# A streaming-encoder layer on one core: x handed over by columns, token sums loaded one by one, eight transpositions ahead of the first projection

## The chip, the core and the metric

One NeuronCore of a Trainium2 chip runs the whole program. TensorE (PE) multiplies, VectorE (DVE) and ScalarE (ACT) convert and do elementwise work, GpSimd (POOL) builds constants and issues some DMAs, SyncE (SP) issues nearly all loads. The metric is the time of one execution on the device in microseconds, the median of several.

## What is computed

One trunk layer on 256 tokens of 2048 columns, all in float32, cut to the lines that matter:

```python
h = rms_norm(x, attn_norm_w)                    # x: (1, 256, 2048)
proj = h @ w_in                                 # 2048 x 5184
hq, hf, hi, hg, c_q, c_kv, k_r = split(proj)    # 4 x 1024, 512, 512, 64
o_a = hgrn2_mixer(hq, hf, hi, hg, ...)          # gated linear recurrence, chunks of 64
o_b = mla_mixer(c_q, c_kv, k_r, ...)            # rms_norm(c_q) @ w_uq, rms_norm(c_kv) @ w_ukv, attention
x = x + concat([o_a, o_b]) @ w_out
gate, up = split(rms_norm(x, ffn_norm_w) @ w_gate_up)   # 2 x 5632
x = x + (silu(gate) * up) @ w_down
```

## The kernel before

**Products in three parts.** Every weight tile is loaded as float32 into `raw`, a ring of four granules. ScalarE rounds it to `w_hi` (line 793, in the later stages line 1013), VectorE takes the rest, `w_lo` = `raw` - `w_hi` (lines 1122 and 1573). The tokens are kept the same way, as `hT_hi` and `hT_lo`, columns on partitions. TensorE then adds hi x hi, hi x lo and lo x hi. For one 128-row tile of weights and 256 tokens these are six products; a granule of the first block (384 columns, two tiles of rows) takes twelve.

**Order.** The first 137 granules go through `w_in`, `w_uq`, `w_ukv` and `w_out`. A table, `SCHEDULE`, gives each side step (transposes, norms, attention) a position among the granules. Each engine walks through the granules and does its part of the steps that stand at a position; ScalarE and VectorE convert granule g + 3 (`LEAD`) at position g. SP loads granule g as soon as the ring slot of granule g - 4 has been converted. Everything on an engine runs in program order, so a wait on one step holds up all behind it.

**The start.** x lies in memory by rows (tokens on partitions). SP loads it in nine pieces, piece p of `PIECES` with its one or two tiles of columns, in turn with the granules 0 to 8 (`load_x`, line 567; weights, line 621); piece 1 and `attn_norm_w` go through ScalarE's queue. TensorE turns each piece by transposes into a `side` bank (`turn_x`, line 1773); ScalarE makes `hT_hi` from the bank with the norm weight as scale (line 840), VectorE makes `hT_lo` (line 1143). The norm weights come as rows and are turned too (`vec`, line 1787): the first 16 at the start, the other 25 at position 19. In the first block (`lat`, 0) the products (line 1751) wait separately for `w_hi` and `hT_hi`, for `hT_lo`, and for `w_lo`. The squares of x (`sq1`) stand at positions 3 to 9 and the root `r_in` at 10 and 11; the latents are multiplied by `r_in` as they leave the accumulation bank (`lat_in`, line 1237). POOL builds masks and other constants after the last piece of x has come (line 711).

**The down projection.** A feed-forward tile is either plain ("S": one granule, twelve products of 512 columns) or paired ("Q": two weight loads that become four granules with 3, 6, 6 and 6 products, and that need sums of token tiles). `DOWN_ITEMS` begins with five S and then repeats Q S S. The token sums were written to memory during the gate-up rounds; POOL loads them back (`sums_in`, line 768), two at a time into `chunk_of(c)`, in the former place of `hT_lo`. ScalarE and VectorE split them behind items 4, 9, 15, 21 and 27. On POOL's queue chunk 0 comes first, then the last turn of the hidden values through memory (`squares`, `hiddenT`, lines 749 and 755), then the other four chunks, each with this wait:

```python
            def sums_in(c):
                pool.wait_ge(s_used, W1 + 2 * c)
                for n, p in enumerate(CHUNKS[c]):
                    pool.dma_start(...)
```

`s_used` counts the granules that TensorE has used up, and `W1` is the first one of the down projection.

Of the kernel before, what the change touches and what calls it, by code (L numbers as in the profile page):

```python
# [27 lines left out]
ALU = mybir.AluOpType  # L28
# [32 lines left out]

V_ATTN, V_FFN, V_QN, V_KVN, V_HG, V_ROWS = 0, KT, 2 * KT, 2 * KT + 4, 2 * KT + 8, 2 * KT + 9
# [107 lines left out]
PAIRED_OF = [[i for i in DOWN_OF[e] if DOWN_ITEMS[i][0] == "Q"] for e in range(2)]  # L170
CONVERTED = AHEAD
# [45 lines left out]
def schedule():  # L217
# [56 lines left out]
    s += [(e + 3, ("r2a",)), (e + 4, ("r2b",))]  # L274
    return sorted(s, key=lambda x: x[0])
# [17 lines left out]
def split_steps_at(position):  # L293

    own = [step for step in steps_at(position) if step[0] != "x"]
    return own + [("x", p) for p, at in enumerate(X_SPLIT) if at == position]


def side_uses(step):

    kind = step[0]
    if kind in ("x", "x2", "lat_t", "o_t"):
        return [(step, "dve")]
    if kind in ("vec", "turn", "probs_t", "join7", "join8"):
        return [(step, "act")]
# [56 lines left out]
def hybrid_layer(nc, x, positions, attn_norm_w, w_in, hgrn_lb, hgrn_norm_w, mla_q_norm_w, w_uq, mla_kv_norm_w,  # L362
                 w_ukv, q_head_norm_w, k_head_norm_w, w_out, ffn_norm_w, w_gate_up, w_down, out):
# [6 lines left out]
    with ExitStack() as ctx:  # L370
# [14 lines left out]
        vec_cols = sb("vec_cols", [P, V_ROWS])  # L385
# [45 lines left out]
        vec_rows = stage[0:KT, 0, 0, 0, 0:P]  # L431
        more_rows = stage[0:V_ROWS - KT, 0, 0, 1, 0:P]
# [62 lines left out]
        s_x = [sem(f"s_x{p}") for p in range(len(PIECES))]  # L495
        s_attn = sem("s_attn")
# [66 lines left out]
        def load_x(engine, p):  # L563

            k, wide = PIECES[p]
            cols = slice(P * k, P * (k + wide))
            engine.dma_start(X[:, :, cols], x_v[:, :, cols]).then_inc(s_x[p], 16)
# [24 lines left out]
        def all_of(v):  # L592
# [3 lines left out]
        small_loads = [(more_rows[r - KT:r - KT + w.shape[1] // P, :], w.rearrange("a (k p) -> (a k) p", p=P))  # L596
                       for r, w in ((V_FFN, ffn_norm_w), (V_QN, mla_q_norm_w), (V_KVN, mla_kv_norm_w),
                                    (V_HG, hgrn_norm_w))]
        small_loads += [(pos_i[:, :], positions[0].rearrange("(t p) -> p t", p=P)),
                        (qw_row[:, :], q_head_norm_w[0].partition_broadcast(P)),  # L600
                        (kw_row[:, :], k_head_norm_w[0].partition_broadcast(P))]
# [6 lines left out]
        def _(sp):  # L608
# [5 lines left out]
            load_x(sp, 0)  # L614
            for g, (b, k, n) in enumerate(GRANULES):
                kind, i, w, c0, cols, rows, _ = BLOCKS[b]
                if g >= RING:
                    slot_free(g)
                src = weights[w][rows[k]:rows[k] + n * P, c0:c0 + cols].rearrange("(k p) c -> p k c", p=P)
                dst = raw[:, g % RING, 0:n * cols].rearrange("p (k c) -> p k c", k=n)  # L620
                sp.dma_start(dst, src).then_inc(s_raw[g % RING], 16)

                for p in X_AFTER.get(g, ()):
                    load_x(sp, p)

                if 0 <= g - 7 < N_SMALL:
                    dst, src = small_loads[g - 7]
                    sp.dma_start(dst, src, allow_slow_non_contiguous=True).then_inc(s_small, 16)
# [51 lines left out]
        def _(pool):  # L680
# [29 lines left out]
            pool.wait_ge(s_x[len(PIECES) - 1], 16)  # L710
# [73 lines left out]
        def _(act):  # L784
# [58 lines left out]
            def step(s):  # L843
                kind, a = s[0], s[1:]
                if kind == "vec":
                    lo, hi = ((0, KT), (KT, V_ROWS))[a[0]]
                    copy(vec_cols[:, lo:hi], filled(s)[:, 0:hi - lo]).then_inc(s_given["act"], 1)
                    act.wait_ge(s_given["act"], GIVEN[USE[s]])
                elif kind == "x":
                    ps, (k, wide) = filled(s), PIECES[a[0]]  # L850
                    split_hi([(hT_hi[:, k + n, :], ps[:, n * SEQ:(n + 1) * SEQ], V_ATTN + k + n) for n in range(wide)])
                elif kind == "sq1":
                    c = a[0]
                    for p, (k, _) in enumerate(PIECES):
                        if k // 4 == c:
                            act.wait_ge(s_x[p], 16)
# [8 lines left out]
                elif kind == "lat_a":  # L865
# [3 lines left out]
                    sums_free(s)  # L869
# [177 lines left out]
            for g in range(FIRST, G0):  # L1047
# [3 lines left out]
                for s in split_steps_at(g):  # L1051
                    step(s)
# [1037 lines left out]
```

## Time and profile before

| | us |
|---|---|
| median of 3 runs | 1115.05 (1113.57 to 1115.18) |
| the profiled execution | 1115.01 |
| its span, first to last instruction | 1113.3 |
| TensorE busy | 1103.5 (99%) |
| VectorE, ScalarE busy | 900.2 (81%), 644.7 (58%) |
| DMA | 230.01 MB, mean 207 GB/s |

A busy TensorE is not yet one at its best pace, since products overlap in the pipeline and their ends are modelled: how long a product really takes is the distance from its start to the next one's. The chain of waits follows the work that ended last back from the end. A wait is put down to what ended it, and idle time of an engine off the chain costs nothing by itself.

### The profile page before, as it was taken

The numbers are of one execution on the slowest core, as the hardware profiler recorded it, in microseconds if no ns is written. First come the engines' busy times: TensorE is split into PE (matmuls) and PEld (weight loads), VectorE is DVE, ScalarE is ACT, GpSimd is POOL, SyncE is SP. The second block draws the span as 40 slices with busy tenths as digits, with TensorE's granted clock in tenths as the row PEclk, the third lists the DMA queues.
The fourth block names the chain that finished last, engine by engine and source line by source line (L and its number), as shares of the span: only waits on it lengthen the run. The fifth ranks groups of instructions, "written<-read, shape, count | busy, mean of one in ns | idle before, by whom it ended". The sixth has DMA issues, their size and how long they took to land.

```text
span 1113.3 us, 15363 instructions
## 1 busy us (share of the span) xinstructions
PE 1103.5 (99%) x5176; PEld 927.6 (83%) x5176; DVE 900.2 (81%) x1234; ACT 644.7 (58%) x910; POOL 61.0 (5%) x154
## 2 busy tenths in 40 slices
PE   8999999999999999999999999999999999999998
PEld 7988888888888888888888888888888878888887
DVE  6688787587876577588988888988988889999887
ACT  7566777668654466365455555554554555655553
POOL 4200000000000000000000000000000020000000
PEclk9999999999999999999999999999999999999999
DMA  8766455554655455767777777787777786666665
GB/s 269 209 187 200 146 169 157 157 162 152 230 183 172 164 176 171 227 218 224 234 236 225 228 233 220 230 240 218 233 237 228 233 290 210 200 215 202 197 205 170
DMA packets 107557, 230.01 MB, mean 207 GB/s; under 512 B 8265, under 2 KB 19314, under 8 KB 107250
## 3 DMA queue, kind: packets, MB, share of 16 engines
q1 hardware_dynamic: 101346, 209.30, 60.3%
q0 software_dynamic: 5856, 19.93, 5.7%
q8 instruction: 28, 0.46, 0.2%
q14 instruction: 23, 0.19, 0.0%
q10 hardware_dynamic: 304, 0.14, 0.0%
HBM read 218.85 MB, written 10.49 MB: 206 GB/s over the span
## 4 chain that ended last, share of the span: by engine, by line
PE 91%; DVE 4%; DMA 2%; ACT 1%; issue 1%; SPq 0%; DVEq 0%; ACTq 0%
PE side L1975 22%; PE main L1731 20%; PE side L1977 11%; PE main L1734 10%; PE side L1945 4%; PE side L1946 4%; PE side L1947 4%; PE main L1945 3%; PE main L1946 3%; PE main L1947 3%; DMA raw<-in_w_down 1%; PE main L1751 1%; PE side L1773 1%; DVE w_lo L1122 1%; PE side L1870 1%
## 5 line engine op out<-in xcount | busy, mean ns | idle before, releaser
L1013 ACT CAST w_hi<-raw 128x1024 fp32r<-128x1024 f32 x245 | 239.8, 984 | 162.8 <-PE side L1975 62.8
L1573 DVE TENSOR_TENSOR w_lo<-raw,w_hi 128x1024 fp32r<-128x1024 f32 x245 | 274.6, 1133 | 17.7 <-ACT w_hi L1013 17.5
L1122 DVE TENSOR_TENSOR w_lo<-raw,w_hi 128x1024 fp32r<-128x1024 f32 (+3 forms) x156 | 178.8, 1156 | 97.1 <-ACT w_hi L793 94.4
L793 ACT CAST w_hi<-raw 128x1024 fp32r<-128x1024 f32 (+3 forms) x156 | 153.4, 993 | 130.2 <-PE main L1731 125.4
L1731 PE MATMUL main<-w_hi,hT_hi 128*128 128x512 f32 (+2 forms) x416 | 161.2, 388 | 0.2 <-issue 0.2
L1734 PE MATMUL main<-w_hi,hT_lo 128*128 128x512 f32 (+2 forms) x416 | 157.6, 380 | 0.0
L1975 PE MATMUL side<-w_hi,hT_hi 128*128 128x512 f32 x400 | 155.6, 389 | 0.0
L1977 PE MATMUL side<-w_hi,hT_lo 128*128 128x512 f32 x400 | 155.6, 389 | 0.0
L1731 PE MATMUL main<-w_lo,hT_hi 128*128 128x512 f32 (+2 forms) x416 | 107.1, 379 | 0.0
L1975 PE MATMUL side<-w_lo,hT_hi 128*128 128x512 f32 x400 | 106.9, 389 | 0.0
L1731 PEld LDWEIGHTS main<-w_hi,hT_hi 128*128 128x128 f32 x416 | 78.2, 188 | 13.2 <-issue 0.4
L1734 PEld LDWEIGHTS main<-w_hi,hT_lo 128*128 128x128 f32 x416 | 78.2, 188 | 12.9
L1731 PEld LDWEIGHTS main<-w_lo,hT_hi 128*128 128x128 f32 x416 | 76.8, 188 | 14.1
L1975 PEld LDWEIGHTS side<-w_lo,hT_hi 128*128 128x128 f32 x400 | 75.1, 188 | 15.6
L1977 PEld LDWEIGHTS side<-w_hi,hT_lo 128*128 128x128 f32 x400 | 75.1, 188 | 15.6
L1975 PEld LDWEIGHTS side<-w_hi,hT_hi 128*128 128x128 f32 x400 | 75.1, 188 | 15.6
L1573 DVE TENSOR_TENSOR w_lo<-last_two,w_hi 128x1024 fp32r<-128x1024 f32 x39 | 47.8, 1225 | 41.1 <-ACT w_hi L1013 41.1
L1013 ACT CAST w_hi<-last_two 128x1024 fp32r<-128x1024 f32 x39 | 41.0, 1052 | 63.9 <-PE side L1975 63.1
L1013 ACT CAST w_hi<-first_two 128x1024 fp32r<-128x1024 f32 x39 | 41.2, 1056 | 58.7 <-PE side L1975 58.1
L1975 PE MATMUL side<-w_hi,aT_hi 128*128 128x512 f32 x184 | 71.6, 389 | 0.0
L1977 PE MATMUL side<-w_hi,aT_lo 128*128 128x512 f32 x184 | 71.6, 389 | 0.0
L1731 PE MATMUL main<-w_hi,mT_hi 128*128 128x512 f32 (+1 forms) x160 | 62.0, 387 | 0.0
(292 smaller groups left out, 1887.5 us busy)
## 6 DMA issues: line engine op xcount, KB each, us to landing
raw<-in_w_gate_up SPq DMA_DIRECT2D x176, 512.0 KB, 4.8
raw<-in_w_down SPq DMA_DIRECT2D x88, 512.0 KB, 4.5
raw<-in_w_in SPq DMA_DIRECT2D x64, 512.0 KB, 4.0
raw<-in_w_out SPq DMA_DIRECT2D x32, 512.0 KB, 3.6
raw<-in_w_in SPq DMA_DIRECT2D x15, 384.0 KB, 5.0
squares<-hiddenT POOLq DMA_DIRECT2D x11, 512.0 KB, 5.3
hiddenT<-squares POOLq DMA_DIRECT2D x44, 128.0 KB, 5.2
raw<-in_w_ukv SPq DMA_DIRECT2D x8, 512.0 KB, 4.0
```

The source lines that it names most:

```text
L793: copy(w_hi[:, slot, 0:n], raw[:, slot, 0:n]).then_inc(s_hi, 1)
L1013: copy(w_hi[:, n % RING, 0:cols], src).then_inc(s_hi, 1)
L1122: tt(w_lo[:, slot, 0:n], raw[:, slot, 0:n], w_hi[:, slot, 0:n].bitcast(F32), ALU.subtract)\
L1573: tt(w_lo[:, n % RING, 0:cols], src, w_hi[:, n % RING, 0:cols].bitcast(F32), ALU.subtract)\
L1731: m = matmul(banks[t][:, 0:cols], hi[:, at[n], tok], rhs, start=(part == "hi" and k == k_first), stop=(part == "lo" and k == last))
L1734: matmul(banks[t][:, 0:cols], lo[:, at[n], tok], rhs, start=False, stop=False)
L1751: m = matmul(banks[t][:, 0:cols], tokens[:, k, t * P:(t + 1) * P], w[:, slot, n * cols:(n + 1) * cols], start=(part == "hi" and k == 0), s ...
L1945: matmul(bank, hi, big, start=first, stop=False)
L1946: matmul(bank, lo, big, start=False, stop=False)
L1947: return matmul(bank, hi, small, start=False, stop=last)
L1975: m = matmul(bank, hi, rhs, start=False, stop=(part == "lo" and (t, half) in last))
L1977: matmul(bank, lo, rhs, start=False, stop=False)
```

## The change

x is handed over a second time, by columns, and the norm weights with it: `columns` is 128 x (41 + 16 * 256), for each partition 41 norm weights and then the 16 tiles of x turned. It is loaded into `x_columns`, which lies where `hT_lo` is written later, tile by tile in the same place. So no transposes of x and of the norm weights are left in front of the latents. The rows of x, which the squares and the end need, are loaded in four quarters behind granules 11, 12, 14 and 16; squares and root move to positions 10 to 17. The latents are copied unscaled, and the scale by `r_in` goes into the squares and the later multiplication. Granule 0 goes through ScalarE's queue. TensorE turns the identity eight times before the first product. In the down projection each token sum has its own wait, `SUMS_FROM`.

```diff
+SUMS_FROM = (0, 0, 4, 8, 13, 19, 25, 31, 37, 43)
...
-X_AFTER = {1: (2,), 2: (3,), 3: (4,), 4: (5,), 5: (6,), 6: (7,), 7: (8,)}
-X_TURNED = (FIRST, -1, 1, 2, 3, 4, 5, 6, 7)
+WARM = 8
+XT_AFTER = {1: (1,), 2: (2,), 3: (3, 4), 4: (5,), 5: (6,), 6: (7,), 7: (8,)}
+X_AFTER = {11: 0, 12: 1, 14: 2, 16: 3}
+SMALL_AFTER = 18
...
-    s = [(FIRST, ("vec", 0))] + [(at, ("x", p)) for p, at in enumerate(X_TURNED)]
-    s += [(2 * c + 3, ("sq1", c)) for c in range(4)]
-    s += [(10, ("r1a",)), (11, ("r1b",)), (19, ("vec", 1))]
+    s = [(at, ("sq1", c)) for c, at in enumerate((10, 12, 13, 15))]
+    s += [(16, ("r1a",)), (17, ("r1b",))]
...
+    s += [(at, ("x", p)) for p, at in enumerate(X_SPLIT)]
...
+        loaded = ctx.enter_context(ExitStack())
+        x_columns = sb("x_columns", [P, GAP + KT * SEQ], F32, loaded)[:, GAP - V_ROWS:]
+        loaded.close()
+        sb("vec_cols", [P, GAP])
+        vec_cols = x_columns[:, 0:V_ROWS]
         hT_lo = sb("hT_lo", [P, KT, SEQ], F32R)
...
+        def load_tokens(p):
             k, wide = PIECES[p]
+            c0, c1 = V_ROWS + SEQ * k if p else 0, V_ROWS + SEQ * (k + wide)
+            nc.sync.dma_start(x_columns[:, c0:c1], columns[:, c0:c1]).then_inc(s_xt[p], 16)
...
-            load_x(sp, 0)
-            for g, (b, k, n) in enumerate(GRANULES):
+            load_tokens(0)
+            for g in range(1, G0):
                 if g >= RING:
                     slot_free(g)
...
+                load_granule(sp, g)
+                for p in XT_AFTER.get(g, ()):
+                    load_tokens(p)
+                if g in X_AFTER:
+                    cols = slice(NB * X_AFTER[g], NB * (X_AFTER[g] + 1))
+                    sp.dma_start(X[:, :, cols], x_v[:, :, cols]).then_inc(s_x[X_AFTER[g]], 16)
...
-            pool.wait_ge(s_x[len(PIECES) - 1], 16)
+            pool.wait_ge(s_x[3], 16)
...
-                pool.wait_ge(s_used, W1 + 2 * c)
                 for n, p in enumerate(CHUNKS[c]):
+                    pool.wait_ge(s_used, W1 + SUMS_FROM[p])
...
-                    ps, (k, wide) = filled(s), PIECES[a[0]]
-                    split_hi([(hT_hi[:, k + n, :], ps[:, n * SEQ:(n + 1) * SEQ], V_ATTN + k + n) for n in range(wide)])
+                    k, wide = PIECES[a[0]]
+                    act.wait_ge(s_xt[a[0]], 16)
+                    split_hi([(hT_hi[:, k + n, :], x_turned(k + n), V_ATTN + k + n) for n in range(wide)])
...
+                    act.wait_ge(s_inv, RMS.index(("r1a",)) + 1)
                     for t in range(NT):
-                        square(latents[i][:, t, :], sumsq[:, t:t + 1])
+                        square(latents[i][:, t, :], sumsq[:, t:t + 1], scale=r_in[:, t:t + 1])
...
-            act.dma_start(vec_rows[0:KT, :], attn_norm_w.rearrange("a (k p) -> (a k) p", p=P)).then_inc(s_attn, 16)
-            load_x(act, 1)
+            load_granule(act, 0)
...
-                        ts(v, v, inv[:, t:t + 1], None, ALU.mult).then_inc(s_lat, 1)
+                        ts(v, v, inv[:, t:t + 1], r_in[:, t:t + 1], ALU.mult, ALU.mult).then_inc(s_lat, 1)
...
-            for g in range(FIRST, 0):
-                for s in steps_at(g):
-                    step(s)
+            pe.wait_ge(s_const, N_IDENT)
+            for _ in range(WARM):
+                transpose(side[SIDE - 1][:, 0:P], ident[:, :], ident[:, :])
```

The order on TensorE at the start of the program, before (`side` banks take transposes, `main` banks the products of the first block):

```order
L1787 MATMUL side<-ident,stage 128x16
L1773 MATMUL side<-ident,X 128x128 x4
L1751 MATMUL main<-w_hi,hT_hi 128x384 x2
L1751 MATMUL main<-w_hi,hT_lo 128x384 x2
L1751 MATMUL main<-w_lo,hT_hi 128x384 x2
L1773 MATMUL side<-ident,X 128x128 x4
```

and now:

```order
L1917 MATMUL side<-ident 128x128 x8
L1763 MATMUL main<-w_hi,hT_hi 128x384 x2
L1763 MATMUL main<-w_hi,hT_lo 128x384 x2
L1763 MATMUL main<-w_lo,hT_hi 128x384 x2
L1763 MATMUL main<-w_hi,hT_hi 128x384 x2
```

The transposes of the norm weights and of x no longer stand between the products.

The order on SP's queue around the first quarters of x, now (before, small loads stood here between the weights, and the rows of x had come with granules 0 to 7):

```order
L568 DMA x_columns<-in_columns 128x512
L580 DMA raw<-in_w_in 128x2x384 x4
L635 DMA X<-in_x 128x2x512
L580 DMA raw<-in_w_in 128x2x384
L635 DMA X<-in_x 128x2x512
L580 DMA raw<-in_w_in 128x2x384 x2
```

The rows of x now come a second time, as 0.52 MB pieces in the stream of weights.

## Rows read from the trace of the kernel before

**Rows 1.** The page's part 1: busy time, share of the span, instructions.
```profile
PE 1103.5 (99%) x5176; PEld 927.6 (83%) x5176; DVE 900.2 (81%) x1234; ACT 644.7 (58%) x910; POOL 61.0 (5%) x154
```

**Rows 2.** Chain of waits, 0 to 26 us: start, us, what.
```profile
2.76 5.84 DMA raw<-in_w_in
...
11.29 1.66 PE main L1751 x8
12.95 0.44 PE side L1773 x4
13.38 2.09 PE main L1751 x12
...
23.08 0.44 PE side L1773 x4
```

**Rows 3.** Timeline, 0 to 16 us: start, us, engine, line, tiles [idle before].
```profile
9.47 0.42 PEld L1773 LDWEIGHTS side<-ident,X 128*128 128x128 f32 x4 [0.72 <-DMA X<-in_x]
...
10.36 0.87 DVE L1143 SCALAR_TENSOR_TENSOR hT_lo<-side,vec_cols,hT_hi 128x256 fp32r<-128x256 f32 x2
...
11.39 0.96 DVE L1122 TENSOR_TENSOR w_lo<-raw,w_hi 128x768 fp32r<-128x768 f32 x1 [0.15 <-ACT w_hi L793]
...
13.29 0.96 DVE L1122 TENSOR_TENSOR w_lo<-raw,w_hi 128x768 fp32r<-128x768 f32 x1 [0.15 <-DVE hT_lo L1143]
```

**Rows 4.** Timeline of DVE, 898 to 918 us.
```profile
902.54 1.23 DVE L1584 TENSOR_TENSOR first_two<-raw 128x1024 f32<-128x1024 f32 x1 [2.79 <-issue]
```

**Rows 5.** Timeline of POOL, 880 to 915 us.
```profile
895.68 3.21 POOL L768 DMA_DIRECT2D hT_lo<-token_sums  x6
```

**Rows 6.** Windows: busy us per engine, then granted PE clock, DMA share, GB/s.
```profile
6.00:8.00 2.00, 2.00 (x10) 1.90 (x9) 1.04 (x2) 0.32 (x1) 0.00 (x0) 1.00 0.90 270
...
10.00:12.00 2.00, 1.78 (x10) 1.36 (x9) 1.85 (x4) 1.71 (x4) 0.00 (x0) 1.00 1.05 375
```

**Rows 7.** Chain of waits, 47 to 49 us.
```profile
47.84 0.17 PE side L1787
48.01 0.35 PE main L1731
48.36 0.15 PE main L1734
```

**Rows 8.** Timelines of POOL and DVE: the last constant, the first use.
```profile
34.45 0.96 POOL L737 MEMSET qTr<- 128x1024 f32 x1
...
72.87 0.16 DVE L1184 CAST pos_f<-pos_i 128x2 f32<-128x2 int32 x1
```

**Rows 9.** Timeline of PE, 904 to 908 and 916 to 919 us.
```profile
904.21 1.07 PE L1975 MATMUL side<-w_lo,aT_hi 128*128 128x512 f32 x4
...
907.46 0.39 PE L1947 MATMUL side<-w_lo,aT_hi 128*128 128x512 f32 x1
...
915.62 1.07 PE L1975 MATMUL side<-w_lo,aT_hi 128*128 128x512 f32 x4
916.53 0.39 PE L1945 MATMUL main<-w_hi,aT_hi 128*128 128x512 f32 x1
...
918.20 0.39 PE L1947 MATMUL side<-w_lo,aT_hi 128*128 128x512 f32 x1
```

**Rows 10.** DMA queues, 900 to 903 us: packets, MB, share (q0 POOL, q1 SP).
```profile
q0 software_dynamic: 248, 0.79, 98.1%
q1 hardware_dynamic: 8, 0.02, 2.4%
```

**Rows 11.** Tile `raw`, loads issued 463 to 870 us, then 894 to 900 us.
```profile
DMA to landing us min/median/max: 3.8/4.9/8.2
...
DMA to landing us min/median/max: 8.3/8.3/9.6
```

**Rows 12.** Timeline of PE, 0 to 16 us.
```profile
6.49 0.84 PE L1751 MATMUL main<-w_lo,hT_hi 128*128 128x384 f32 x2
...
8.56 0.51 PE L1751 MATMUL main<-w_lo,hT_hi 128*128 128x384 f32 x2
```

More of the change, by code:

```diff
@@ L290, in steps_at @@
     return [step for p, step in SCHEDULE if p == position]
-def split_steps_at(position):
-    own = [step for step in steps_at(position) if step[0] != "x"]
-    return own + [("x", p) for p, at in enumerate(X_SPLIT) if at == position]
 def side_uses(step):
     kind = step[0]
-    if kind in ("x", "x2", "lat_t", "o_t"):
+    if kind in ("x2", "lat_t", "o_t"):
         return [(step, "dve")]
-    if kind in ("vec", "turn", "probs_t", "join7", "join8"):
+    if kind in ("turn", "probs_t", "join7", "join8"):
         return [(step, "act")]
@@ L494, in hybrid_layer @@
         s_tlo = sem("s_tlo")
-        s_x = [sem(f"s_x{p}") for p in range(len(PIECES))]
-        s_attn = sem("s_attn")
+        s_xt = [sem(f"s_xt{p}") for p in range(len(PIECES))]
+        s_x = [sem(f"s_x{c}") for c in range(4)]
         s_small = sem("s_small")
@@ L561, in taken, with x_turned, load_granule @@
             return NT * (b // 2 + 1)
-        def load_x(engine, p):
+        def load_tokens(p):
             k, wide = PIECES[p]
-            cols = slice(P * k, P * (k + wide))
-            engine.dma_start(X[:, :, cols], x_v[:, :, cols]).then_inc(s_x[p], 16)
+            c0, c1 = V_ROWS + SEQ * k if p else 0, V_ROWS + SEQ * (k + wide)
+            nc.sync.dma_start(x_columns[:, c0:c1], columns[:, c0:c1]).then_inc(s_xt[p], 16)
+        def x_turned(k):
+            return x_columns[:, V_ROWS + SEQ * k:V_ROWS + SEQ * (k + 1)]
+        def load_granule(engine, g):
+            b, k, n = GRANULES[g]
+            _, _, w, c0, cols, rows, _ = BLOCKS[b]
+            src = weights[w][rows[k]:rows[k] + n * P, c0:c0 + cols].rearrange("(k p) c -> p k c", p=P)
+            dst = raw[:, g % RING, 0:n * cols].rearrange("p (k c) -> p k c", k=n)
+            engine.dma_start(dst, src).then_inc(s_raw[g % RING], 16)
         def bank(n):
@@ L1050, in _ @@
                     convert(n % RING, loads(n), n, granule_size(n))
-                for s in split_steps_at(g):
+                for s in steps_at(g):
                     step(s)
@@ L1212, in step @@
                 if kind == "x":
-                    ps, (k, wide) = filled(s), PIECES[a[0]]
-                    split_lo(s, [(hT_lo[:, k + n, :], ps[:, n * SEQ:(n + 1) * SEQ], hT_hi[:, k + n, :],
-                                  V_ATTN + k + n) for n in range(wide)])
+                    k, wide = PIECES[a[0]]
+                    dve.wait_ge(s_thi, SPLIT[s] + 1)
+                    for n in range(k, k + wide):
+                        ins = stt(out=hT_lo[:, n, :], in0=x_turned(n), scalar=vec_cols[:, V_ATTN + n:V_ATTN + n + 1],
+                                  in1=hT_hi[:, n, :].bitcast(F32), op0=ALU.mult, op1=ALU.subtract)
+                    ins.then_inc(s_tlo, 1)
                 elif kind in ("r1a", "r2a"):
@@ L1651, in _ @@
                     convert(n % RING, n, granule_size(n))
-                for s in split_steps_at(g):
+                for s in steps_at(g):
                     step(s)
@@ L1777, in step @@
                 kind, a = s[0], s[1:]
[L1778 to L1792 removed]
+                if kind == "x2":
                     c, j = a
@@ L2081 @@
     rows = np.concatenate([np.arange(P), np.arange(SEQ - 1, P - 1, -1)])
+    laid = {**inputs, "x": inputs["x"][:, rows], "positions": inputs["positions"][:, rows]}
+    norms = [inputs[f"{n}_w"][0].reshape(-1, P).T
+             for n in ("attn_norm", "ffn_norm", "mla_q_norm", "mla_kv_norm", "hgrn_norm")]
+    x_columns = laid["x"][0].T.reshape(KT, P, SEQ).transpose(1, 0, 2).reshape(P, KT * SEQ)
+    laid["columns"] = np.concatenate(norms + [x_columns], axis=1)
     for name in _INS:
-        a = np.ascontiguousarray(inputs[name][:, rows] if name in ("x", "positions") else inputs[name])
+        a = np.ascontiguousarray(laid[name])
         arrays[f"in_{name}"] = a
```

64 lines of the change are left out of this document (18 added, 46 removed).

## The prediction

> **What bounds the kernel now.** I read the busy shares first. TensorE has work in 1103.5 us of the 1113.3 us span, 99% [rows 1]: what shortens this kernel either takes instructions off TensorE or closes one of the few places where it stands still. The table of waits then says where those are: in the whole middle TensorE waits for almost nothing, and the longest wait behind the start is one for `w_lo` from VectorE, early in the down projection. So I looked at three places: the start, up to the end of the first projection block; position 19, with the second turn of norm weights; and the first 40 us of the down projection.
>
> At the start the chain [rows 2] goes through the load of weight granule 2 (issued 2.76, landed 8.60), its conversion, and the first product with the low tokens at 11.29. From 12.95 on it is TensorE alone: 0.44 for four transposes of x, 2.09 for the granule's twelve products, and so on, five times (12.95 to 23.08). VectorE explains 11.29: it made `w_lo` of granule 2 and then `hT_lo` (0.87 from 10.36) [rows 3]. In the down stage TensorE stands still twice, each time at the second granule of a paired item; in front of the first VectorE waited 2.79 us for a weight load [rows 4], while POOL's token-sum loads were in flight: eight in one burst from 895.68, the first six 0.5 us apart [rows 5].
>
> The profiled execution took 1115.01 us, 0.04 below the median of the runs, so the sum below holds against the median as well. A measurement can tell about 0.2%, that is 2.2 us, from no change.
>
> **The change part by part.**
>
> *Transposes of x on TensorE: -2.2.* All 32 go. Those of pieces 0 to 3 lay before granule 2's products, where the loads set the pace. Those of pieces 4 to 8 are on the path: five times 0.44 [rows 2]. After that a granule costs TensorE 2.09 instead of 2.53. What is late next? VectorE needs 1.90 per granule (11.39 to 13.29, no wait but the 0.15 between its own steps) [rows 3]. The loads need 393,216 B of weights and 262,144 B of x, 1.75 us at the 375 GB/s of this stretch [rows 6]. ScalarE needs two activations of the same sizes as before, and its squares of x are moved out of the stretch. So TensorE stays the slowest of the four, by 0.19 us: a thin cover. If VectorE lost another 0.2 us per granule, six granules would cost 1.2.
>
> *The second turn of norm weights: -0.37.* On the chain it takes 0.17, and the product behind it 0.35 where a product of this block takes 0.15 [rows 7]: 0.17 + 0.35 - 0.15. Nothing replaces it, since the weights come with the first load of x.
>
> *The first granules: -0.7.* Granules 0 and 1 are done early both ways. What decides is when granule 2 has `hT_lo`. Before, 1.32 MB had been ordered up to the end of granule 2 (8 KB of weights, x pieces 0 to 2, granules 0 to 2), landed at 8.60 [rows 2]; then came the cast, `w_lo` and `hT_lo`, and the products at 11.29: 2.69 in all. Now piece 2 is ordered behind granule 2, and up to its end there are 1.33 MB. If the bytes come at the same rate, granule 2 lands a little before 8 and piece 2 at about 8.65. Behind piece 2 only its activations and `hT_lo` remain, 0.87 each at most [rows 3], and two hand-overs, 1.8 in all, so 10.45; behind granule 2 it is 7.9 + 2.69 = 10.6. The later of the two gives 10.6, a gain of 0.7. Ends: if piece 2 lands as late as piece 3 did (9.47, [rows 3]) the products start at 11.27 and nothing is gained; if the wider pieces of x (2 KB per partition, before 1 KB in two parts) come faster, 8.0 and a gain of 1.4 is possible. I take the same-bytes value.
>
> *Eight transposes of the identity: 0.* They wait only for the identity and run while the first loads are under way; granule 0 cannot start before its load. Four transposes take 0.44 on the chain [rows 2]; eight at half that pace take 1.8 us.
>
> *x by rows, loaded again: 0.* Four quarters of 0.52 MB behind granules 11, 12, 14 and 16, in SP's queue in front of weights. At 375 GB/s [rows 6] they cost 5.6 us of transfer. The cover is the ring of four granules and converted granules up to three ahead of TensorE, and each square waits for a quarter that stands in the queue before the granule converted just before. Without the cover this is the slower rival below.
>
> *POOL, the root, the latents: 0.* POOL's constants now wait for the last quarter, ordered behind granule 16 and not 7: nine granules, an estimated 19 us later. Before, they were ready at 35.4 and first needed at 72.87 [rows 8], so the slack shrinks to some 15 us and holds. The latents are copied unscaled; root and squares take the scale in the same instructions.
>
> *Token sums by need: -1.43.* The two stands cost: from 904.21 to 907.46 lie nine products, at 0.228 each (915.62 to 916.53, four) 2.05, taken 3.25, so 1.20; from 915.62 to 918.20 again nine, taken 2.58, so 0.53 [rows 9]. Together 1.73. The change asks for sums 4 to 9 one by one from 13 granules on, and only two loads stay behind the moves of `hiddenT`. In 900 to 903 POOL's queue moved 0.79 MB and SP's 0.02 MB [rows 10]: the weights stood still while sums flowed. Against this: in the ten gate-up rounds, where the same moves of `hiddenT` run with no burst behind them, a weight load also takes up to 8.2 us, against 8.3 to 9.6 here [rows 11]. The load that ends the first wait took 8.3; closing the whole stand needs 7.1. The second goes with the burst. I leave 0.3 of the first: 1.73 - 0.3. Ends: 0.53 (the first stays) and 1.73. Each sum has time to land: the tightest, sum 3, is asked for after 8 granules and split behind 12, and 33 products (7.5 us) lie between.
>
> The Trainium skill, "DMA: Bandwidth & Descriptors", section "Queues, rings and completion order", says that each DMA engine goes round the queues that have work, packet by packet. By that, SP's queue would keep its share beside POOL's, the first stand would have another cause and stay, and the time would be 1111.2; the rows of 900 to 903 do not look like turns.
>
> Sum: 1115.01 - 2.2 - 0.37 - 0.7 - 1.43 = **1110.3 us**.
>
> **The rivals.**
>
> *A. The start gives nothing, or costs* (chance 0.17). For it: the first loads were slow and I know one start only; TensorE will idle between granules 1 and 2 for longer than now, since no transposes of x stand there. Without the 0.7 the time is 1111.0. If TensorE is also at its low clock when granule 2 comes, two products take 0.84, as at 6.49, instead of 0.51, as at 8.56 [rows 12], six times 0.33 or 2.0: 1113.0. (The granted clock is shown as 1.00 in both stretches [rows 6]; the pace at 6.49 is that of the 1.2 GHz level all the same.) Against it: the low pace was over before 8.56 and did not return in the waits that followed.
> The Trainium skill, "TensorE: Matmul & The Clock Gate", "Part 4: PE-mode transpose", says that transposes do not count as work for the clock; then the eight would buy nothing and this case gets likelier. No run here shows it yet.
>
> *B. The first stand in the down stage stays* (0.20): the moves of `hiddenT` alone hold the load up, as in the gate-up rounds [rows 11]. Then 1.20 - 0.3 = 0.9 less is won: 1111.2.
>
> *C. The rows of x stop the ring* (0.04), the slower side. Between the first quarter and granule 17 SP orders 2.10 MB of x and 2.29 MB of weights. TensorE takes six times 2.09 for these granules and has a ring of four in front, 8.4: 20.9 us. At 210 GB/s it just fits. The whole gain of 4.7 is gone at 4.39 MB / 25.6 us = 171 GB/s, and at 158 GB/s the time is 1117.2. Against it: 375 GB/s [rows 6].
>
> **How the numbers follow.** Forecast 0.59, A 0.17, B 0.20, C 0.04. Forecast and B are faster by over 0.2% (limit 1112.8), A for the most part: 0.59 + 0.20 + 0.07 = 0.86. The other 0.10 of A lies around the limit: within 0.2%. C: slower, 0.04. The range reaches down to the good ends (0.7 more at the start, 0.3 in the down stage: 1109.3) and up to A with half of its clock price and part of B, 1112.5.
>
> **What would show it.** In the new profile: no transposes of x before the latents'; granules 3 to 8 at 2.09 each without gaps; the second block's first product (line 1731 before) about 3 us earlier; no DMA wait of ScalarE between granules 11 and 18; POOL's loads of sums spread over some 70 us, weight loads near 900 back at 5 to 7 us, and products of the paired items near 905 and 917 at 0.228 without a wait. Wrong would be: products of granule 2 at the low pace or later than 11.3, or a wait for `w_lo` in the down stage as long as now.

## The result, and the profile after

The change made the kernel slower. Its median is 1119.33 us (7 runs, 1117.98 to 1124.01), that of the kernel before on the same chip 1114.37 (7 runs, 1113.41 to 1115.28): ratio 1.0049, 95% interval 1.0034 to 1.0063. The forecast was 1110.3. The profiled execution took 1119.63, its span is 1117.9, 4.6 more than before.

To find where 4.6 us come from, I set the start of the same granule's first product in the two traces side by side (granules counted through the program from 0):

| granule | before, us | after minus before |
|---|---|---|
| 2, in the first block | 10.34 | -0.95 |
| 8, the first block's last | 25.45 | -2.60 |
| 20, in the third block | 49.81 | -2.60 |
| 22, behind the first latent's transposes | 54.12 | -1.17 |
| 153, first of the ten gate-up rounds | 459.16 | +0.06 |
| 350, near their end | 872.73 | +5.95 |
| 364, ahead of the first stand of the down stage | 905.24 | +5.55 |
| 372, behind the second | 919.13 | +3.97 |
| 478, the last | 1106.82 | +4.70 |

So four things happened: a gain of 2.6 at the start, a loss of 1.4 at once between granules 20 and 22, a steady loss of 7.1 from granule 22 to 350, and a gain of 1.6 at the two stands. Two smaller steps make up the rest. Between granules 350 and 364 the distance falls by 0.4; it falls by 0.5 as well in the kernel before with two tiles moved that cost nothing (below), so that is scatter. Behind granule 372 another 0.7 is lost: there the token sums stand in `hT_lo`'s place, and the products that load them read 395 to 397 ns, before 389.

**The steady loss.** Part 1 of the page after, against [rows 1]: TensorE issues 26 instructions fewer and is busy 6.2 us longer.

```profile
PE 1109.7 (99%) x5150; PEld 927.5 (83%) x5150; DVE 901.2 (81%) x1234; ACT 645.2 (58%) x908; POOL 59.6 (5%) x154
```

The groups of products of the gate-up rounds, 462 to 880 us, by form, show which. First the kernel before (line, engine, output <- weights tile and tokens, shapes, count | busy us, mean ns of one | idle):

```profile
L1975 PE MATMUL side<-w_hi,hT_hi 128*128 128x512 f32 x400 | 155.6, 389 | 0.0
L1977 PE MATMUL side<-w_hi,hT_lo 128*128 128x512 f32 x400 | 155.6, 389 | 0.0
L1975 PE MATMUL side<-w_lo,hT_hi 128*128 128x512 f32 x400 | 106.9, 389 | 0.0
...
L1946 PE MATMUL side<-w_hi,hT_lo 128*128 128x512 f32 x115 | 44.7, 389 | 0.0
...
L1946 PE MATMUL main<-w_hi,ff_sums_lo 128*128 128x512 f32 x60 | 23.3, 389 | 0.0
```

The same groups after:

```profile
L1976 PE MATMUL side<-w_hi,hT_lo 128*128 128x512 f32 x395 | 155.5, 394 | 0.0
L1974 PE MATMUL side<-w_hi,hT_hi 128*128 128x512 f32 x395 | 154.7, 392 | 0.0
L1974 PE MATMUL side<-w_lo,hT_hi 128*128 128x512 f32 x392 | 104.9, 389 | 0.0
L1945 PE MATMUL side<-w_hi,hT_lo 128*128 128x512 f32 x113 | 44.9, 397 | 0.0
...
L1945 PE MATMUL main<-w_hi,ff_sums_lo 128*128 128x512 f32 x60 | 23.6, 393 | 0.0
```

No row has idle time, so nothing is waited for. Products with `hT_lo`, and those around them in the order, take 3 to 8 ns longer. (`side<-w_lo,hT_hi` come four in a row, and those stay at 389.) The rows of `ff_sums` are slower too, and read the same in the kernel before with one line moved (below), where these tiles stay in their place: the disturbance outlasts the product that loads `hT_lo`. From one such product of a paired item on, at 645.07 us, the starts are 241, 237, 234, 236, 224, 231, 235, 229, 232, 231 and 227 ns apart, and then 226 to 227, which is the distance of all of them before. None of these instructions is in the diff. What the diff does move is where `hT_lo` lies: the 192 bytes of `vec_cols` now stand ahead of it. It starts at byte 74048 of each partition and not at 73856; the old start is 577 x 128, the new one is 64 bytes beyond a multiple of 128. `X` and `ident`, next to it, moved with it.

**The loss at granule 22.** The timeline of TensorE around the first latent's transposes, after:

```profile
50.12 0.75 PE L1743 MATMUL main<-w_lo,hT_hi 128*128 128x320 f32 x4
52.12 1.07 PE L1785 MATMUL side<-ident,lat 128*128 128x128 f32 x8 [1.26 <-DVE lat L1255]
```

Before, TensorE did not wait here. The chain of waits that leads to 52.12, after (start, us, what):

```profile
25.07 8.38 DMA raw<-in_w_in
...
37.47 5.99 DMA raw<-in_w_in
43.48 0.73 ACT w_hi L804
...
46.79 0.82 ACT hlf L826 x2
...
50.43 1.56 DVE lat L1255 x2
```

Weight loads take 6 to 8 us, and behind the cast at 43.48 stand the root and the latent's squares and scaling. The timeline of ScalarE, after, gives what its casts waited for the loads:

```profile
26.73 0.83 ACT L804 CAST w_hi<-raw 128x768 fp32r<-128x768 f32 x1 [2.73 <-DMA raw<-in_w_in]
...
43.48 0.73 ACT L804 CAST w_hi<-raw 128x640 fp32r<-128x640 f32 x1 [2.45 <-DMA raw<-in_w_in]
```

Between 20 and 45 us there are six such waits, 9.5 us in all, before two, 1.8. The windows of 26 to 34 us fit this (busy us per engine, granted clock, DMA share, GB/s), first before, then after: the DMA engines are full.

```profile
26.00:34.00 8.00, 8.00 (x48) 8.00 (x47) 4.97 (x8) 6.12 (x15) 7.24 (x18) 1.00 0.81 253
```

```profile
26.00:34.00 8.00, 8.00 (x47) 8.00 (x47) 2.95 (x4) 4.27 (x8) 0.00 (x0) 1.00 1.04 371
```

The end of the chain is slower for another reason. VectorE scaled the latent in 0.88 us before, and takes 1.56 now. POOL's constants now wait for the last quarter of x, so POOL's last two fills, done at 35.4 before, have moved beside this step. Timelines of VectorE before and of POOL after:

```profile
50.79 0.88 DVE L1243 TENSOR_SCALAR lat<-lat,stat 128x512 f32<-128x512 f32 x2
```

```profile
48.97 1.39 POOL L747 MEMSET hS<- 128x1536 f32 x1
50.29 0.95 POOL L748 MEMSET qTr<- 128x1024 f32 x1
```

The first of the two scaling instructions, begun at 50.43, ends at 51.52, just behind the second fill (51.25), and takes 1.09 us; the second, with no fill beside it, takes 0.53.

**The start.** Timeline of TensorE, after, against [rows 2, 12]:

```profile
1.58 1.97 PE L1917 MATMUL side<-ident 128*128 128x128 f32 x8 [1.58 <-POOL ident L705]
4.90 1.01 PE L1763 MATMUL main<-w_hi,hT_hi 128*128 128x384 f32 x2 [1.35 <-ACT w_hi L804]
...
7.63 0.84 PE L1763 MATMUL main<-w_hi,hT_lo 128*128 128x384 f32 x2
...
9.39 1.62 PE L1763 MATMUL main<-w_hi,hT_hi 128*128 128x384 f32 x4 [0.28 <-ACT hT_hi L851]
10.81 0.95 PE L1763 MATMUL main<-w_hi,hT_lo 128*128 128x384 f32 x4
...
12.31 0.86 PE L1763 MATMUL main<-w_hi,hT_hi 128*128 128x384 f32 x4
...
14.42 0.86 PE L1763 MATMUL main<-w_hi,hT_hi 128*128 128x384 f32 x4
```

Granules follow each other 2.1 us apart from 12.31, without gaps. But the pace of the 1.2 GHz level (0.84 for two products) still holds at 7.63, where before two took 0.52 from 8.20 on, and goes on into granule 2.

**The down stage.** VectorE's wait for the paired weights [rows 4], POOL's first loads and the last [rows 5], TensorE's rows for the two stands [rows 9], after:

```profile
906.73 1.23 DVE L1596 TENSOR_TENSOR first_two<-raw 128x1024 f32<-128x1024 f32 x1 [1.35 <-issue]
```

```profile
900.26 0.56 POOL L779 DMA_DIRECT2D hT_lo<-token_sums  x1
904.45 0.56 POOL L779 DMA_DIRECT2D hT_lo<-token_sums  x1 [3.63 <-PE main L1946]
...
964.57 0.54 POOL L779 DMA_DIRECT2D ff_sums_lo<-token_sums  x1 [9.71 <-PE side L1946]
```

```profile
909.89 1.07 PE L1974 MATMUL side<-w_lo,aT_hi 128*128 128x512 f32 x4
...
911.93 0.39 PE L1946 MATMUL side<-w_lo,aT_hi 128*128 128x512 f32 x1
...
920.14 1.07 PE L1974 MATMUL side<-w_lo,aT_hi 128*128 128x512 f32 x4
...
922.18 0.39 PE L1946 MATMUL side<-w_lo,aT_hi 128*128 128x512 f32 x1
```

Nine products take 2.04 both times, before 3.25 and 2.58: both stands are gone, and the loads of sums are spread over 64 us.

### The profile page after: what moved, and what is told of

The parts are those of the page before. It is cut to its first block, busy times and chain, and to the rows that moved or that the text cites. A ratio compares the mean times of both kernels' runs of the same rounds, so it can differ in the third digit from the quotient of the medians.

```text
span 1117.9 us, 15281 instructions
## 1 busy us (share of the span) xinstructions
PE 1109.7 (99%) x5150; PEld 927.5 (83%) x5150; DVE 901.2 (81%) x1234; ACT 645.2 (58%) x908; POOL 59.6 (5%) x154
## 4 chain that ended last, share of the span: by engine, by line
PE 94%; DMA 3%; DVE 2%; ACT 1%; issue 0%; SPq 0%; DVEq 0%; ACTq 0%
PE side L1974 24%; PE main L1743 20%; PE side L1976 12%; PE main L1746 10%; PE side L1945 4%; PE side L1944 4%; PE side L1946 4%; PE main L1945 3%; PE main L1944 3%; PE main L1946 3%; DMA raw<-in_w_in 2%; DVE w_lo L1128 1%; PE side L1785 1%; PE side L1869 1%; ACT w_hi L804 0%
```

## The experiments

The theory was: `hT_lo`'s start sets the pace of the products that load it as weights, 7 us. Rivals: `X` or `ident`, which moved too; or the handing over by columns itself.

### Where hT_lo lies

**The changed kernel with hT_lo on a multiple of 128** (called mended below). Nothing behind the statistics moves.

```diff
-GAP = 48
+GAP = 64
-        sb("vec_cols", [P, GAP])
+        front = sb("vec_cols", [P, GAP])
-        stat = sb("stat", [P, 72])
-        sb("gap", [P, 8])
+        stat = sb("stat", [P, 64])
-        polish = stat[:, 62:70]
+        polish = front[:, 0:8]
```

> The changed kernel with hT_lo, X and ident 64 bytes further on in each partition, so that hT_lo starts at byte 74112 (579 x 128, as before at 577 x 128) where the change put it at 74048, 64 bytes beyond a multiple of 128. Nothing else moves but nine small columns of statistics. Theory (the place of hT_lo sets the pace of the products that load it as weights): in the gate-up stage the groups with hT_lo and the groups beside them go back from 392 to 397 ns to 389, the round of twenty granules back by some 0.6 us, and the whole by 6 to 8 us: 1111.5 to 1113.5 us. Rival (the values or the handing over of x by columns are at fault, not the place): 392 to 397 ns stay and the time is 1119.3 us.

**The kernel before with one line moved.**

```diff
+        vec_cols = sb("vec_cols", [P, V_ROWS])
         hT_lo = sb("hT_lo", [P, KT, SEQ], F32R)
         X = sb("X", [P, NT, D])
         ident = sb("ident", [P, P])
-        vec_cols = sb("vec_cols", [P, V_ROWS])
```

> The kernel before with one line moved: vec_cols is allotted ahead of hT_lo and not behind ident. hT_lo, X and ident then start where they do in the changed kernel, 64 bytes beyond a multiple of 128; every other tile and every instruction stays. Theory: the products with hT_lo go from 389 to 392 to 397 ns and the time rises by 6 to 8 us to 1120.5 to 1122.5 us. Rival (the place is not the cause): 1114.4 us and 389 ns.

**The kernel before, hT_lo alone, then X and ident alone.** `few` and `few2` are 64 bytes each and hold statistics that were in `stat` (cut to [P, 40]). First:

```diff
+        few = sb("few", [P, 16])
         hT_lo = sb("hT_lo", [P, KT, SEQ], F32R)
+        few2 = sb("few2", [P, 16])
         X = sb("X", [P, NT, D])
```

> The kernel before with hT_lo alone 64 bytes beyond a multiple of 128 (statistics of 64 bytes put ahead of it and 64 behind it); X and ident stay on multiples of 128. Theory (weights loaded from hT_lo): as in the run with one line moved, 1120.5 to 1122.5 us. Rival (X or ident, which VectorE, ScalarE and the transpositions read, are what costs): 1114.4 us here.

Second:

```diff
         hT_lo = sb("hT_lo", [P, KT, SEQ], F32R)
+        few = sb("few", [P, 16])
         X = sb("X", [P, NT, D])
         ident = sb("ident", [P, P])
+        few2 = sb("few2", [P, 16])
```

> The kernel before with X and ident alone 64 bytes beyond a multiple of 128 (64 bytes of statistics between hT_lo and X, 64 behind ident); hT_lo stays at byte 73856. Theory (weights loaded from hT_lo): 1114.4 us, all products at 389 ns. Rival (X or ident): 1120.5 to 1122.5 us here.

**hT_lo alone by 32 and by 96 bytes.** As the first of these two, `few` with 8 columns and `few2` with 24, or the other way round.

> The kernel before with hT_lo alone 32 bytes beyond a multiple of 128 (byte 73888). If any start off a multiple of 128 costs the same (the 512 bytes of one partition's weights then lie in five stretches of 128 and not four): 1122 us, as at 64 bytes. If the cost goes with the distance, or a start off a multiple of 64 costs more: another time, below 1119 or above 1125 us.

> The kernel before with hT_lo alone 96 bytes beyond a multiple of 128 (byte 73952). If the cost goes by the largest power of two that divides the start (64: 7.8 us, 32: 15.2 us), 96 costs as 32 does: 1129.5 us. If it goes by the distance to the next multiple of 128, or by that from the last, 96 costs as 32 or more than 64 does less: 1118 us or so where the cost falls with the distance, as from 15.2 at 32 to 7.8 at 64.

Measured (products: how many TensorE issued in the same stretch, 460 to 881 us, by the windows view; stage: from granule 153 to granule 350, against 413.57 before):

| kernel | hT_lo starts at | off 128 | products | stage | median us | ratio to before, 95% |
|---|---|---|---|---|---|---|
| before | 73856 | 0 | 1858 | | | |
| changed | 74048 | 64 | 1833 | +5.89 | 1119.33 | 1.0049 (1.0034 to 1.0063) |
| changed, mended | 74112 | 0 | 1859 | +0.01 | 1111.91 | 0.9983 (0.9973 to 0.9992) |
| before, line moved | 74048 | 64 | 1831 | +5.89 | 1122.38 | 1.0078 (1.0064 to 1.0091) |
| before, hT_lo alone | 73920 | 64 | 1837 | +4.53 | 1122.23 | 1.0076 (1.0059 to 1.0093) |
| before, X and ident | 73856 | 0 | 1859 | +0.00 | 1114.11 | 1.0000 (0.9990 to 1.0009) |
| before, hT_lo alone | 73888 | 32 | 1814 | +9.87 | 1129.79 | 1.0135 (1.0119 to 1.0151) |
| before, hT_lo alone | 73952 | 96 | 1824 | +7.67 | 1125.28 | 1.0093 (1.0076 to 1.0111) |

The groups of the gate-up rounds of the kernel before with the one line moved read as those of the changed kernel:

```profile
L1977 PE MATMUL side<-w_hi,hT_lo 128*128 128x512 f32 x392 | 154.3, 394 | 0.0
L1975 PE MATMUL side<-w_hi,hT_hi 128*128 128x512 f32 x392 | 153.6, 392 | 0.0
L1975 PE MATMUL side<-w_lo,hT_hi 128*128 128x512 f32 x390 | 104.4, 389 | 0.0
```

and those of the changed kernel, mended, as those before:

```profile
L1973 PE MATMUL side<-w_hi,hT_hi 128*128 128x512 f32 x396 | 154.0, 389 | 0.0
L1975 PE MATMUL side<-w_hi,hT_lo 128*128 128x512 f32 x396 | 154.0, 389 | 0.0
```

At 32 bytes the products of the same rounds are slower still, the four in a row too:

```profile
L1979 PE MATMUL side<-w_hi,hT_lo 128*128 128x512 f32 x384 | 152.6, 398 | 0.0
L1977 PE MATMUL side<-w_hi,hT_hi 128*128 128x512 f32 x384 | 152.0, 396 | 0.0
L1977 PE MATMUL side<-w_lo,hT_hi 128*128 128x512 f32 x384 | 103.6, 392 | 0.0
```

This settles it: one moved line costs the kernel before 0.78%, a start on a multiple of 128 gives the changed kernel 7.4 us back (1119.33 to 1111.91), `hT_lo` moved alone costs as much in the median, and `X` and `ident` moved alone cost nothing. In the stage alone `hT_lo` by itself gives 4.53 of the 5.89 us. The rest is open: its start there, 73920, is another one (192 bytes beyond a multiple of 256, 74048 is 64 beyond), and `X` and `ident` did not move with it. Both good starts lie 128 bytes beyond a multiple of 256; a multiple of 256 was not tried. The price does not go by one rule that I had: 96 bytes cost neither as 32 nor less than 64, but 10.7 us between 15.2 and 7.8 (medians). How the load disturbs the products is open: the weight loads themselves read 188 ns before and after.

### The wait at the latents

With `hT_lo` in place the changed kernel is 0.17% faster, not the 4.7 us of the forecast. The next runs start from it and look at the wait near 50 us. (`e` is the end of a latent's block; positions count granules.)

**The first latent turned two granules later.**

```diff
-        s += [(e + 1, ("lat_a", i)), (e + 2, ("lat_b", i))] + [(e + 5, ("lat_t", i, n)) for n in range(2)]
+        s += [(e + 1, ("lat_a", i)), (e + 2, ("lat_b", i))] + [(e + 7 - 2 * i, ("lat_t", i, n)) for n in range(2)]
```

> The kernel with hT_lo at byte 74112 (1111.9 us), and the transpositions of the first latent two granules later, ahead of granule 24 instead of 22; their first use is the block that begins at granule 33. Theory (the wait of 1.02 us at granule 22 takes back that much of the start, since the squares, the root and the scaling of the latent come after casts that wait for the ring): the wait goes and the time is 1110.9 us. Rival (the ring itself is behind, the next product that waits for a cast takes the place): 1111.9 us, with waits of TensorE for w_lo or w_hi between 50 and 60 us.

**hgrn_lb loaded later.**

```diff
             pool.wait_ge(s_x[3], 16)
-            pool.dma_start(lb[:, :, :], hgrn_lb[:, 0:GW].partition_broadcast(P)).then_inc(s_lbin, 16)
...
             done(pool.memset(qTr[:, :, :, :], 0.0))
+            pool.dma_start(lb[:, :, :], hgrn_lb[:, 0:GW].partition_broadcast(P)).then_inc(s_lbin, 16)
```

> The kernel with hT_lo at byte 74112 (1111.9 us), with only the load of hgrn_lb (512 KB, near 35 us) moved behind the making of the masks, to near 50 us. Theory (the quarters of x are what makes the ring late): the wait of 1 to 2.5 us of TensorE near 50 us stays within its scatter, 1111 to 1112.5 us. Rival (the load of hgrn_lb is what makes the load for granule 20 late): the cast of granule 20 begins near 40 us and not at 42.3, the wait goes and the time is 1110 to 1110.9 us.

**Quarters of x apart, the root and the first latent later.**

```diff
-X_AFTER = {11: 0, 12: 1, 14: 2, 16: 3}
+X_AFTER = {11: 0, 14: 1, 17: 2, 20: 3}
...
-    s = [(at, ("sq1", c)) for c, at in enumerate((10, 12, 13, 15))]
-    s += [(16, ("r1a",)), (17, ("r1b",))]
+    s = [(at, ("sq1", c)) for c, at in enumerate((10, 13, 16, 19))]
+    s += [(20, ("r1a",)), (21, ("r1b",))]
...
-        e = END[("lat", i + 1)]
+        e = END[("lat", i + 1)] + 4 * (i == 0)
```

> The kernel with hT_lo at byte 74112 (1111.9 us), with the four quarters of x by rows three loads apart (after loads 11, 14, 17 and 20, not 11, 12, 14 and 16), their squares and the root four granules later, and the squares, root, scaling and transposition of the first latent four granules later as well (transposed ahead of granule 26). Theory (the quarters of x, 2 MB in 15 us beside the granules, make the ring late, and the casts that wait for it hold up the latent's chain behind them): casts near 42 us wait less than 1 us for their load, TensorE stands still for under 0.3 us between 45 and 60 us, and the time is 1.0 to 2.0 us less, 1110 to 1111 us. Rival (some other load keeps the ring late, as hgrn_lb, which now lands later still): a wait of 1 to 2.5 us stays, at another granule, and the time is 1111.9 us.

**All of it**, with `WARM = 13`.

> The kernel with hT_lo at byte 74112, with the spread quarters and the later latent of chain_late, the later load of hgrn_lb of lb_late, and thirteen transpositions of the identity in place of eight. If the three act apart: a lead over the kernel before of 4.0 to 4.4 us at granule 20 (the thirteen gave 4.41 beside 3.78), kept up to the down stage, and 2.2 us of the token sums beyond it: 1107.5 to 1108.5 us. If the wait in the first blocks only moves: 1110 to 1111 us.

**x by rows almost without bytes.**

```diff
-                    cols = slice(NB * X_AFTER[g], NB * (X_AFTER[g] + 1))
+                    cols = slice(NB * X_AFTER[g], NB * X_AFTER[g] + 32)
...
-                        square(X[:, t, c * NB:(c + 1) * NB], sumsq[:, 4 * t + c:4 * t + c + 1])
+                        square(hT_hi[:, 4 * c + 2 * t:4 * c + 2 * t + 2, :].rearrange("p k t -> p (k t)").bitcast(F32), sumsq[:, 4 * t + c:4 * t + c + 1])
```

> The kernel with hT_lo at byte 74112, with only the first 32 of each quarter's 512 columns of x by rows loaded (0.13 MB in place of 2.1), and the squares taken of hT_hi, 512 columns each as before. So the root of x is left out, and another number stands in its place; all instructions on ScalarE and VectorE keep their sizes and places. Theory (the bytes of x by rows make the ring late and with it the latent's chain): no wait of ScalarE for a weight load between 20 and 45 us over 0.5 us, TensorE waits less than 0.2 us at the transpositions of the latent near 50 us, lead over the kernel before at granule 23 some 3.5 us and 1110.3 to 1110.9 us. Rival (the chain is late by its place behind the casts, with or without these bytes, since TensorE comes 2.6 us earlier): a wait of 1 us or more stays, 1111.9 us.

Measured (distance to the kernel before at two granules, on both sides of the wait):

| kernel | granule 20 | granule 30 | TensorE's wait | median us | ratio, 95% |
|---|---|---|---|---|---|
| mended | -3.58 | -2.38 | 1.02 | 1111.91 | 0.9983 (0.9973 to 0.9992) |
| turned later | -3.78 | -2.05 | 1.48 | 1110.15 | 0.9962 (0.9949 to 0.9976) |
| hgrn_lb later | -3.39 | -1.61 | 1.59 | 1111.71 | 0.9976 (0.9966 to 0.9985) |
| quarters apart, chain later | -4.34 | -3.36 | 0.72 | 1109.74 | 0.9959 (0.9943 to 0.9975) |
| all of it | -4.55 | -4.52 | none | 1109.32 | 0.9958 (0.9944 to 0.9972) |
| x almost without bytes | -4.07 | -3.30 | 0.59 | 1109.05 | 0.9948 (0.9931 to 0.9964) |

The first run's wait moved by one granule, as its rival had it, but not for want of weights: VectorE scales the latent (two instructions, 2.51 us, beside POOL's fills from 49.08 to 51.34) ahead of the `w_lo` that TensorE now asks for. Its timelines of VectorE and TensorE:

```profile
49.57 2.51 DVE L1254 TENSOR_SCALAR lat<-lat,stat 128x512 f32<-128x512 f32 x2
```

```profile
52.96 0.39 PE L1742 MATMUL main<-w_hi,hT_hi 128*128 128x320 f32 x1 [1.48 <-DVE w_lo L1127]
```

Loading `hgrn_lb` later does not take TensorE's wait away (1.59), but it does take the late load near 42 us away: the cast there begins at 41.40 and waits for no load. What holds the chain in this run is the scaling, 3.14 us beside POOL's fills from 49.01 to 51.26. Almost without the bytes of x the wait shrinks from 1.02 to 0.59 and does not go, and ScalarE still waits three times for a load (1.1 to 1.3 us): neither side of that expectation held. Here POOL's fills stand beside an earlier step of the chain, one that took 0.17 us before. VectorE and POOL:

```profile
45.72 2.05 DVE L1238 TENSOR_SCALAR stat<-stat 128x2 f32<-128x2 f32 x1 [1.00 <-ACT hlf L825]
```

```profile
45.47 1.38 POOL L746 MEMSET hS<- 128x1536 f32 x1
46.79 0.95 POOL L747 MEMSET qTr<- 128x1024 f32 x1
```

In all ten traces with POOL's constants behind the last quarter of x, a `TENSOR_SCALAR` of this chain overlaps these fills and ends 0.02 to 0.3 us behind one of them. What it loses by that is 0.6 us in the changed kernel and the mended one, and 1.5 with the latent turned later, 2.1 with `hgrn_lb` later, 2.1 with the quarters apart and 1.9 almost without the bytes of x; in these four it is more than TensorE's whole wait. So three things make the wait: late loads, the chain's place behind the casts, now that TensorE comes 3 to 4 us earlier, and POOL's fills. No run moved the fills alone, so what each is worth is not shown.

With the chain later, the quarters apart and `hgrn_lb` later, TensorE turns the latent without a wait:

```profile
56.81 1.03 PE L1784 MATMUL side<-ident,lat 128*128 128x128 f32 x8
```

Which of the three moves did most was not separated, and the ratios of the last three rows lie within each other's intervals. The scatter is large: the kernel of the last part below is the same program up to the down stage as the mended one, waited 2.59 here (1.5 of it lost beside POOL's fills) and lost 4.1 us between granules 20 and 30, where the mended one lost 1.2.

### The eight transpositions

Both on top of the first latent turned later; `WARM = 0` and `WARM = 13`.

> As late_t, without the eight transpositions of the identity. Theory A (they do nothing for the pace of the first products): low pace of 0.32 us a product until about 10.5 us as with them, time as late_t within 0.3 us. Theory B (they count as work for the clock): the low pace lasts longer by up to 2 us and the time rises by 0.5 to 1 us.

> As late_t, with thirteen transpositions of the identity, which fill TensorE up to the first product at 4.85 us. Theory A (transpositions of the identity do nothing): low pace until about 10.5 us, time as late_t. Theory B (they count, and the gap of 1.3 us ahead of the first product is what sent the clock back): full pace near 7 us, granule 3 begins up to 0.9 us earlier and the time is up to 0.9 us less than that of late_t.

Timelines of TensorE, with eight (that kernel itself), none, and thirteen:

```profile
1.58 1.97 PE L1916 MATMUL side<-ident 128*128 128x128 f32 x8 [1.58 <-POOL ident L704]
...
10.25 0.85 PE L1762 MATMUL main<-w_hi,hT_lo 128*128 128x384 f32 x4
```

```profile
10.54 0.88 PE L1762 MATMUL main<-w_hi,hT_lo 128*128 128x384 f32 x4
```

```profile
1.58 3.04 PE L1916 MATMUL side<-ident 128*128 128x128 f32 x13 [1.58 <-POOL ident L704]
...
6.84 0.51 PE L1762 MATMUL main<-w_hi,hT_hi 128*128 128x384 f32 x2
```

With eight and with none the pace of the 2.4 GHz level comes at the same products, near 10.3. With thirteen, which reach up to the first product, it comes at 6.84, and granule 8 starts 4.05 earlier than before, beside 3.41 and 3.09. (The granted clock is shown as 1.00 all along.) One trace of each says little by itself: over the seven traces with eight the first product at the higher pace (the next starts within 0.2 us) begins between 8.08 and 11.07. With thirteen it begins at 6.84 and, in the run of "all of it", at 5.32, earlier than in the other fourteen traces (8.03 at the earliest). So transpositions up to the first product do count here; a gain from eight followed by 1.3 us of nothing cannot be told from this scatter. The Trainium skill, "TensorE: Matmul & The Clock Gate", "Part 4: PE-mode transpose", says that they do not count as work; the run with thirteen speaks against it. In the median nothing is left of the gain: 1110.56 (0.9961, 0.9948 to 0.9975) with thirteen, 1110.15 with eight (0.9962). Without any it is 1111.69 (0.9974, 0.9965 to 0.9984), but that execution's loss at the latents was 3.1 us, within the scatter told above.

### The token sums alone

The mended kernel with the loads as before:

```diff
-SUMS_FROM = (0, 0, 4, 8, 13, 19, 25, 31, 37, 43)
+SUMS_FROM = tuple(p // 2 * 2 for p in range(10))
```

> The kernel with hT_lo at byte 74112 (1111.9 us), with the token sums loaded as before, two pairs at a time as soon as the earlier of the chunk's tiles is free. Theory (the term of the prediction, 1.43 us, which the trace of the changed kernel gave as 1.7): stands of 1.2 and 0.5 us near 902 and 913 us are back and the time is 1113.3 to 1113.6 us. Rival (loading by need is worth nothing once the rest is moved): 1111.9 us.

Measured: 1113.72 us, near what was expected; ratio 0.9990 (0.9981 to 1.0000), beside 0.9983 by need: not told apart by the intervals. In the profiles the difference between granules 364 and 372 is 2.35 us (+0.29 to +0.99 with the old loads, -3.16 to -4.81 by need). All sixteen traces together say more. The second stand (granules 370 to 372) was 0.55 to 0.57 shorter than before in all nine with sums by need, and in one of the six others. The first (364 to 366) went in six of those nine and also, wholly or nearly, in three of the six with the old loads; in the run of "all of it" VectorE waited almost as long for its weights as before [rows 4]:

```profile
897.15 1.23 DVE L1595 TENSOR_TENSOR first_two<-raw 128x1024 f32<-128x1024 f32 x1 [2.59 <-issue]
```

## Why the prediction was wrong

**The step that failed** is one that the sum lacks. "The change part by part" costs instructions, bytes and waits; the five lines that put `vec_cols` ahead of `hT_lo` got no term, as if a tile's place were free. They cost 7.1 us from granule 22 to 350 and 0.7 behind granule 372, and made the sign wrong. No rival held it either, and the row that I took as the bound, TensorE at 99% [rows 1], said only that TensorE is full, not that its pace can change.

**"x by rows, loaded again: 0" and "POOL, the root, the latents: 0"** failed as well: 1.4 us in this trace, 1.2 to 4.1 in the others that left the chain at its place and loaded x in full. "No DMA wait of ScalarE between granules 11 and 18" was wrong, there were waits up to 2.7. Rival C had the cause but looked for it at the wrong place: it reckoned when TensorE would lack weights, which it never did after the change, and not when the side chain behind the late casts would be late. The step took the latents' instructions as free because their sizes stayed; their due time came 2.6 us nearer. And it weighed POOL's later constants only against their first use at 72.87, not against what VectorE would be doing beside POOL's fills.

**Transposes of x: -2.2.** From granule 3 to granule 8 the mended kernel gained 1.91, the changed one 1.78. I had taken 0.44 of the chain for each; between starts it is 0.38.

**The second turn of norm weights: -0.37.** From granule 16 to 20 the gain is 0.35 and, mended, 0.37. Right.

**The first granules: -0.7.** Granule 3 starts 0.83 earlier, near the forecast, and 1.31 in the mended kernel; over the seven traces with eight transpositions it is 0.82 to 2.06, so the hit is partly luck. The first products of granule 2 with the low tokens came at 10.81, 0.48 earlier than before. Part of rival A came true: granule 2 began 0.95 earlier, at the pace of the lower level, and its first four products took 1.42 to the next, where before it was 0.95. The price was 0.5 in this trace, not 2.0.

**Eight transposes of the identity: 0.** Not contradicted: no gain from them can be told from the scatter of the start.

**Token sums by need: -1.43.** Both stands went in the profile, 1.58 between granules 364 and 372. The second goes with the sums: it is gone in all nine traces with sums by need and there in five of the six others. For the first the forecast's own doubt, rival B, stands: it went and came back with either loading, so what makes it is the timing of the weight load among the moves of `hiddenT` and the sums, and it is not settled which.

The rule of the Trainium skill weighed there, "DMA: Bandwidth & Descriptors", "Queues, rings and completion order" (the queues take turns), is neither borne out nor excluded by this.

## What to carry to other kernels

When a diff adds or moves a tile, write down the start byte of every tile behind it, before and after, modulo 128, and give a term to those that TensorE loads as weights. Compare the mean time of one product between two profiles before looking for waits: a full engine can be slower. And when the main engine gets ahead, move the side chains' due times with it: a step that was free is free only up to its old slack. When constants on another engine come later, look at what they now stand beside, not only at when they are needed.

## What was not expected of the hardware

- The start of the weights in their partition changes the pace of products. Off a multiple of 128 bytes by 64, 96 and 32, with 128 columns of float32 weights and 512 moving columns, the kernel takes 7.8, 10.7 and 15.2 us more (medians against 1114.4 to 1114.6). A group of products with or beside such loads reads up to 8, 7 and 11 ns more than 389. The Trainium skill, "TensorE: Matmul & The Clock Gate", "Step-by-step: what each phase is for", has the load of the next weights on a read port of its own, so that it takes nothing from the running product; on a multiple of 128 the trace does not speak against that; off it the products around such loads are slower, by a way that is open. The section "Operand start alignment" of "SBUF — State Buffer" tells which starts are legal and says that it timed nothing.
- A VectorE `TENSOR_SCALAR` beside POOL's fills of `hS` and `qTr` ended only behind a fill, in all ten traces where the two met: 2.05 us on 128x2 elements, where 0.17 was taken before.
- Thirteen transpositions without a gap behind them brought the higher pace at 6.84 and 5.32 us; with eight and a gap of 1.3 us it came between 8.08 and 11.07.
- The lowest median of a kernel that computes the layer in full has `hT_lo` in place, the three moves and thirteen transpositions: 1109.32 us, 0.42% (0.28% to 0.56%) under the kernel before. The ratios of three others lie within that interval.
